# First mixer of a hybrid decoder: ten units multiply columns of x before the root mean square is known

## What is computed

```
def rmsnorm(x, g):
    y = x * rsqrt(mean(x * x, axis=-1, keepdims=True) + 1e-6)
    return y * g

def token_mixer(hn, ...):                      # hn = rmsnorm(x, ln1_g[l])
    p = hn @ w_in                              # 1024 x 5648
    xc, gb_c, gc_c, q, k, v, g_out, a_low, gate_a, gate_b = split(p)
    y_a = gb_c * short_conv(gc_c * xc, conv_w)             # three taps over the tokens
    log_a = log_sigmoid(a_low @ w_a2 + b_a) / 16
    o = gla(q * 64 ** -0.5, k, v, log_a)                   # 4 heads, chunks of 64 tokens
    y_b = rmsnorm(o, gla_norm_g) * silu(g_out)
    return (sigmoid(gate_a) * (y_a @ w_branch[0])
            + sigmoid(gate_b) * (y_b @ w_branch[1])) @ w_out
```

## Time and profile before

| what | value |
|---|---|
| median of 3 runs | 1408.72 us (1408.44 to 1408.95) |
| the profiled execution's own time | 1408.48 us |
| its span in the trace | 1406.7 us |
| TensorE busy | 1394.4 us, 99% |
| VectorE, ScalarE, GpSimd busy | 440.0, 301.6, 135.3 us |
| HBM | 462.7 MB moved, mean 329 GB/s |

### The profile page before, as it was taken

One profiled execution on the slowest core, in us unless ns is written; L12 is line 12 of the kernel. 1 busy time (PEld: TensorE's weight loads), 2 busy tenths in 40 slices (PEclk: granted clock), 3 DMA queues, 4 the chain that ended last, 5 costly groups with the idle time before them and its releaser, 6 DMA issues.

```text
span 1406.7 us, 34725 instructions
## 1 busy us (share of the span) xinstructions
PE 1394.4 (99%) x16039; PEld 870.3 (62%) x16039; DVE 440.0 (31%) x724; ACT 301.6 (21%) x425; POOL 135.3 (10%) x167
## 2 busy tenths in 40 slices
PE   9999999999999999999999999999999999999997
PEld 7999999999999983353353354354354344344344
DVE  6775775555777563110110110110110110110121
ACT  6554454444646430000000000000000000000000
POOL 2650000000463000000000000000000000000000
PEclk9999999999999999999999999999999999999999
DMA  9755566666565549999999999999999999999995
GB/s 329 253 180 181 180 195 195 207 204 190 173 201 195 192 160 358 417 418 419 417 419 419 416 419 411 412 420 410 412 421 410 413 420 408 414 421 408 421 420 202
DMA packets 132014, 462.73 MB, mean 329 GB/s; under 512 B 8531, under 2 KB 66545, under 8 KB 117538
## 3 DMA queue, kind: packets, MB, share of 16 engines
q1 hardware_dynamic: 126290, 449.87, 82.4%
q0 software_dynamic: 2448, 7.94, 1.5%
q10 hardware_dynamic: 3136, 2.75, 0.6%
HBM read 455.68 MB, written 4.86 MB: 327 GB/s over the span
## 4 chain that ended last, share of the span: by engine, by line
PE 96%; DVE 2%; issue 0%; DMA 0%; ACT 0%; POOL 0%; SPq 0%; POOLq 0%; DVEq 0%
PE banks L1602 95%; PE banks L1765 1%; DMA x<-in_x_dram 0%; DVE w_lo L819 0%; PE banks L1637 0%; DVE mem L1078 0%; POOL ors L1555 0%; DVE mem L855 0%; DVE mem L1115 0%; ACT mem L670 0%; PE banks L1867 0%; PE banks L1735 0%; PE banks L1798 0%; ACT mem L577 0%; DVE mem L1108 0%
## 5 line engine op out<-in xcount | busy, mean ns | idle before, releaser
L1602 PE MATMUL banks<-mem 128*32 128x448 f32 (+2 forms) x11712 | 878.4, 462 | 0.1
L1602 PEld LDWEIGHTS banks<-mem 128*32 128x32 f32 (+1 forms) x11712 | 381.5, 110 | 494.6 <-issue 377.1
L819 DVE TENSOR_TENSOR w_lo<-mem,w_hi 128x1024 fp32r<-128x1024 f32 x178 | 224.1, 1279 | 112.5 <-ACT w_hi L553 111.3
L1438 DVE TENSOR_TENSOR mem<-mem,banks 128x448 f32<-128x448 f32 x48 | 26.9, 616 | 716.2 <-PE banks L1602 716.2
L1602 PE MATMUL banks<-xt_hi,w_hi 128*128 128x256 f32 x832 | 230.1, 277 | 0.0
L1602 PE MATMUL banks<-xt_lo,w_hi 128*128 128x256 f32 x832 | 228.8, 275 | 0.0
L1602 PE MATMUL banks<-xt_hi,w_lo 128*128 128x256 f32 x832 | 228.8, 275 | 0.0
L553 ACT CAST w_hi<-mem 128x1024 fp32r<-128x1024 f32 x178 | 184.3, 1048 | 159.1 <-PE banks L1602 156.9
L1602 PEld LDWEIGHTS banks<-xt_hi,w_hi 128*128 128x128 f32 x832 | 159.6, 192 | 1.1 <-issue 0.3
L1602 PEld LDWEIGHTS banks<-xt_lo,w_hi 128*128 128x128 f32 x832 | 159.7, 192 | 0.3
L1602 PEld LDWEIGHTS banks<-xt_hi,w_lo 128*128 128x128 f32 x832 | 159.7, 192 | 0.0
(11 more groups left out here) (228 smaller groups left out, 703.3 us busy)
## 6 DMA issues: line engine op xcount, KB each, us to landing
mem<-in_eg_dram SPq DMA_DIRECT2D x128, 896.0 KB, 13.1
mem<-in_eu_dram SPq DMA_DIRECT2D x128, 896.0 KB, 12.9
mem<-in_ed_dram SPq DMA_DIRECT2D x112, 1024.0 KB, 15.2
mem<-in_w_in_dram SPq DMA_DIRECT2D x38, 1024.0 KB, 5.5
mem<-in_fg_dram SPq DMA_DIRECT2D x11, 1024.0 KB, 5.3
mem<-in_fu_dram SPq DMA_DIRECT2D x11, 1024.0 KB, 5.3
mem<-in_fd_dram SPq DMA_DIRECT2D x11, 1024.0 KB, 4.9
mem<-in_w_br_dram SPq DMA_DIRECT2D x8, 1024.0 KB, 5.5
```

Of the source, the lines that this page charges most:

```text
L819: nc.vector.tensor_tensor(w_lo[:, q % H, :], src, w_hi[:, q % H, :].bitcast(F32), ALU.subtract).then_inc(lo_done, 1)
L1438: nc.vector.tensor_tensor(h, h, by_pair(bank[3 + g]), ALU.mult).then_inc(ehf_done, 1)
L1602: return nc.tensor.matmul(out, lhs, rhs, start=first, stop=last, skip_group_check=True)
```

## The change

A second input `xt` holds x transposed on the host, eight blocks of 128 channels by 256 tokens, with the gain of the norm ahead. Its columns and the eight 256 KB parts of v's weights are loaded first, interleaved; the rows of x are loaded after the chunk of q. For l == 0, ten units (v, alow, q, k, xc0, xc1, gc0, gc1, gb0, gb1) multiply `x0_hi` and `x0_lo`, the split of x times gain, without r. r is made from the rows of x meanwhile, spread over the partitions by two matmuls into bank 7 (`spread_root`, between the halves of unit q) and copied to `rs_row`. It enters where the banks are read: v on ScalarE by r per partition; alow, q, k on VectorE times `rs_row`; xc0 and xc1 on VectorE times r squared (for xc and gc); the taps' result once more times r (for gb). ScalarE no longer reads q, k, xc0, xc1 in layer 0. For the units from go on, VectorE makes the normed columns (`normed`, eight multiplications of 128 x 256), ScalarE casts them (`normed_high`), VectorE subtracts (`normed_low`). TensorE's warm-up is eleven matmuls of zeros; the gain's spreading and the transposes of x go. The small parameter loads of GpSimd are issued after the second part of v has landed, the large ones after r.

```diff
@@ SyncE
+            columns(0, 0, KT + 2 * SEQ)
+            value_rows(0, 1, value_in[0])
+            value_rows(1, 1, value_in[1])
+            columns(1, KT + 2 * SEQ, KT + 4 * SEQ)
+            value_rows(2, 1, value_in[2])
+            value_rows(3, 1, raw_in[0])
+            columns(2, KT + 4 * SEQ, KT + 8 * SEQ)
+            value_rows(4, 2, value_in[3])
+            value_rows(6, 2, raw_in[1])
...
+                    if l == 0 and n == 2:
+                        for t in range(TB):
+                            sp.dma_start(x[:, t, :], x_d[0, t * P:(t + 1) * P, :]).then_inc(x_in[t], 16)
@@ ScalarE
+                    for kk in range(KT):
+                        weighed_high(kk)
+                        half_split(kk)
...
+                    until(H)
+                    norm_squares(0, (0, 2))
+                    until(H + 4)
...
+                if l == 0:
+                    after(2)
+                    normed_high(0)
+                    after(4)
+                    normed_high(1)
+                    after(5)
@@ VectorE
+                    for kk in range(KT):
+                        weighed_low(kk)
+                        half_low(kk)
...
                     until(H)
+                    own_half(0)
+                    own_half(1)
+                    dve.wait_ge(rs_full, 1)
+                    step(nc.vector.tensor_copy(rs_row, bank[7][:, 0:SEQ]))
...
+                    nc.vector.tensor_tensor(own_al, al_turned, rs_turned[0:2 * RANK, :, :], ALU.mult).then_inc(al_done, 1)
+                    step(nc.vector.tensor_tensor(rs_squared, rs_row, rs_row, ALU.mult))
+                    until(H + 2)
...
+                if l == 0:
+                    until(H + 3)
+                    src = full(l, "q")
+                    for h in range(HP):
+                        ins = nc.vector.scalar_tensor_tensor(...)
+                    ins.then_inc(q_done, 1)
+                    until(H + 4)
...
                 if l == 0:
+                    after(1)
+                    per_token(kT, full(l, "k"), rs_row).then_inc(k_done, 1)
+                    after(2)
+                    normed(0)
+                    after(3)
+                    for n in range(2):
+                        after(4 + n)
+                        per_token(cv[:, 2 * n:2 * n + 2, :], full(l, f"xc{n}"), rs_squared).then_inc(xc_done, 1)
+                        if n == 0:
+                            normed(1)
...
                 for n in range(2):
+                    if l == 0:
+                        normed_low(n)
                     after(6 + n)
...
+                if l == 0:
+                    step(nc.vector.tensor_tensor(cv[:, :, :], cv[:, :, :], rs_row.unsqueeze(1).to_broadcast([P, CB, SEQ]),
+                                                 ALU.mult))
@@ TensorE
-            keep_warm(3)
...
+            keep_warm(11)
             for l in range(DEPTH):
...
+                    for kk in range(KT):
+                        first_values(kk)
+                    low_rank(claim(l, "alow"), l, (x0_hi, x0_lo))
...
+                    channels(claim(l, "q"), base + 4, of=(x0_hi, x0_lo), between=spread_root)
```

More of the change, by code:

```diff
@@ L431, in unit_rows, with columns, value_rows @@
                 return rows(w_in_d[l], 0, KT, col, 256)
[L433 to L437, removed]
+            def columns(n, first, end):
+                sp.dma_start(g_xt[:, first:end], xt_d[:, first:end]).then_inc(xt_in[n], 16)
+            def value_rows(k0, nk, landed):
+                dst = raw(k0 // 4, k0 % 4 * 512, 512 * nk).rearrange("p (k n) -> p k n", k=nk)
+                sp.dma_start(dst, rows(w_in_d[0], k0, nk, C_V, 512)).then_inc(landed, 16)
+            columns(0, 0, KT + 2 * SEQ)
[7 more added lines that the diff above has]
+            value_rows(6, 2, raw_in[1])
             for l in range(DEPTH):
@@ L632, in _ @@
                 nc.scalar.activation(eb[:, :, :], bb[:, :, :], ACT.Exp, scale=1.0 / TAU).then_inc(eb_done, 1)
[L633 to L642, removed]
+                if l == 0:
[4 more added lines that the diff above has]
+                    after(5)
+                else:
+                    after(2)
+                    src = full(l, "q")
+                    nc.scalar.mul(halves(qT[:, :, :]), unturned(src[:, :], HP), DK ** -0.5).then_inc(q_done, 1)
+                    after(3)
+                    src = full(l, "k")
+                    nc.scalar.copy(halves(kT[:, :, :]), unturned(src[:, :], HP)).then_inc(k_done, 1)
+                    for n in range(2):
+                        after(4 + n)
+                        src = full(l, f"xc{n}")
+                        nc.scalar.copy(halves(cv[:, 2 * n:2 * n + 2, :]), unturned(src[:, :], 2)).then_inc(xc_done, 1)
                 for h in range(HP):
@@ new lines, in normed, with normed_low @@
+                    def normed(half):
+                        for kk in range(4 * half, 4 * half + 4):
+                            ins = nc.vector.scalar_tensor_tensor(out=x_cols[:, kk, :], in0=x_cols[:, kk, :],
+                                                                 scalar=g_cols[:, kk:kk + 1], in1=rs_row[:, :],
+                                                                 op0=ALU.mult, op1=ALU.mult)
+                        ins.then_inc(xn_made, 1)
+                    def normed_low(half):
+                        kk = 4 * half
+                        dve.wait_ge(xn_h, half + 1)
+                        nc.vector.tensor_tensor(xt_lo[:, kk:kk + 4, :], x_cols[:, kk:kk + 4, :],
+                                                xt_hi[:, kk:kk + 4, :].bitcast(F32), ALU.subtract).then_inc(xn_l, 1)
@@ L1639, in transposes, with channels @@
                 ins.then_inc(turned, 1)
-            def channels(out, q0, blocks=2, counts=(None, None), ready=None):
+            def channels(out, q0, blocks=2, counts=(None, None), ready=None, of=(xt_hi, xt_lo), between=None):
                 for half in range(2):
+                    if half and between is not None:
+                        between()
                     w = piece(q0 + half, counts[half])
```

228 lines of the change are left out of this document (129 added, 99 removed).

## The result

| | median of the runs | profiled execution | its span |
|---|---|---|---|
| before | 1408.47 us (1408.12 to 1408.95, 9 runs) | 1408.48 us | 1406.7 us |
| changed | 1412.94 us (1412.28 to 1413.59, 9 runs) | 1413.59 us | 1411.8 us |

The ratio is 1.0029, with a 95% interval of 1.0021 to 1.0038. The changed kernel is 4.5 us slower. The forecast was 1410.2, the range 1405.2 to 1414.0: the time is inside the range and 2.7 us above the point. It is above 1411.5, the prediction's bound for "slower", which had a chance of 0.32; "same" had 0.54.

What follows compares the result with a forecast made beforehand. TensorE, busy 99% of the span, was taken as the bound. A 4.7 us head start would be spent on VectorE's longer list, leaving TensorE 1.5 us late: 1408.48 + 1.5 = 1410.0, plus 0.24 for the median: 1410.2 us; range 1405.2 to 1414.0.

Steps and rivals of the forecast that it cites:

- same: Whole kernel: time neither below 1405.9 us (faster) nor above 1411.5 us (slower), chance 0.54.
- The start: Kernel start: first product at 5.7 us instead of 10.98, k starting at 26.3 instead of 31.05.
- head start: From the bias product z on: TensorE starts k 4.7 us sooner than in the kernel before.
- VectorE's list: First mixer, z to go's third piece: VectorE's old work, low parts, new work and waits run from 26.3 to 73.9.
- The wait before go's third piece: TensorE at go's third piece: one wait of some 5 us on the low part of piece 22.
- rival C: Start: r comes late, or landings or a low TensorE clock delay it; 1 to 3 us more, 1412.2, chance 0.11.
- The second chain: GpSimd, ScalarE and conv branch before the transposes: low part at 87.1, TensorE at 87.2; no further cost, no cover left.
- A: First mixer: VectorE keeps pace and the head start survives; 1404.0 with all of it, 1406.3 with half, chance 0.17.
- B: Second head pair's differences and taps: GpSimd and VectorE hold each other up, second exponential at 85, 1413.7, chance 0.15.
- D: Kernel start: the change gains nothing there, k no sooner than 29, VectorE's list 3 us later, 1413, chance 0.04.

Runs made afterwards that it cites:

- e1_warm: Changed kernel with 18 matmuls of zeros on TensorE between go's second and third pieces, filling its wait: 1410.44 us, ratio 1.0014 to the kernel before.
- e4_dose6: Kernel before with six extra, unused VectorE multiplications of 128 x 1024 behind the first mixer's taps: 1415.49 us, ratio 1.0049.
- e6_dose6_warm: Kernel before with e4_dose6's six extra VectorE multiplications plus 18 matmuls of zeros ahead of go's third piece: 1413.04 us, ratio 1.0033.
- e2_order: Changed kernel with ScalarE's two casts of x moved behind the casts of pieces 13 and 17: 1407.19 us, ratio 0.9990 to the kernel before.
- e7_tail: e5_both with VectorE's list behind the taps put in the order in which TensorE needs it: 1404.15 us, ratio 0.9973 to the kernel before.
- e4_dose4: Kernel before with four extra, unused VectorE multiplications of 128 x 1024 behind the first mixer's taps: 1410.70 us, ratio 1.0022.
- e3_late: Changed kernel with go multiplying columns without r (applied in ScalarE's silu) and all of `normed` behind the taps: 1408.00 us, ratio 0.9996 to the kernel before.
- e5_both: Changed kernel with e2_order's casts, e3_late's go, early `normed`, later `normed_low`, and GpSimd's chain started sooner: 1406.02 us, ratio 0.9984 to the kernel before.

## Why the prediction was right where it was, and what it missed

**The start: right.** Forecast: first product at 5.7, step 4 of v at 12.1, z's end at 26.3. The profiled execution had 6.50, 13.11 and 27.2, 0.8 to 1.0 us later, with TensorE standing for v's weights (L964): step 4's landed at 11.7 instead of 10.7. In the profiled executions of the five variants of the change z ended at 26.3 to 26.7. So a head start of 4.4 to 4.7 us is the usual one; 3.9 is this execution's, whose own time was 0.65 above the median. r cost TensorE next to nothing: its spreading began at 22.82, right behind a matmul that had started at 22.71.

**VectorE's list: right.** Forecast 47.6 us from z to the start of piece 22's low part (73.9 - 26.3), measured 47.3. Most terms stand one by one: two waits on ScalarE of 2.0 forecast, 2.06 measured; the eight multiplications 4.0 forecast, 2.30 + 1.66 measured; the reads 0.44 forecast, 0.38 measured; the taps' last product 1.33, within the 1.2 to 1.4. Others were off and cancelled: the fourteen low parts took 19.2 us and not 18.1, the wait behind the exponential 1.2 and not 0.8, while the taps took 7.3 and not 7.7 and the eight reads 3.0 and not 3.5. The wait before go's third piece was there: 4.5 us of the 5.3 that TensorE stood behind z in the first 100 us.

**The step that failed** is the sentence "so it stands some 6 us in all ... It goes on at 75.4 instead of 73.9: 1.5 us later than before". The time of the stand was priced, and what the stand does to the speed afterwards was not. TensorE goes on at 1.2 GHz, and two pieces of go that take 5.2 us take 8.2. By the trace the 4.9 us at 85.07 are 75.84 - 73.9 = 1.9 of lateness, where 1.5 was forecast, and 3.0 of clock, where nothing was. By the medians the 4.5 us are 2.0 (e1_warm over the kernel before) and 2.5 (the changed kernel over e1_warm). Without the fall, e1_warm came to 1410.44, 0.2 from the forecast of 1410.2 (part of this closeness is luck: the forecast added 0.24 for the median of three runs, which nine runs put at 1408.47, 0.01 below the profiled execution); e4_dose6 and e6_dose6_warm show 2.45 us, much the same, in the kernel before. The rows to see it by were there: the earlier trace rows showed 0.54 us for a matmul of zeros at the start, over twice the later 0.216, and the prediction used the lower level for rival C, at the start alone, and not behind a stand of its own making. The Trainium skill has the rule (TensorE: Matmul & The Clock Gate, HAM oscillation — how this bites in real kernels): a wait on data that is long enough between bursts of matmuls makes TensorE start the next burst at the lower clock. This trace agrees: 4.48 us of standing, then 0.50. It was the rule that spoke against this change, and the prediction weighed another one.

**The second chain: right, and without effect.** Forecast: GpSimd's last difference at 81, the low part at 87.1. Measured 81.1 and 87.3, by ScalarE's and VectorE's timelines of the changed kernel:

```profile
81.12 1.70 ACT L695 ACTIVATE mem<-mem 128x1792 f32<-128x1792 f32 x1 [14.63 <-POOL mem L1636]
```

```profile
86.07 1.22 DVE L1154 TENSOR_TENSOR area<-mem,area 128x1024 fp32r<-128x1024 f32 x1
```

But TensorE came to the transposes at 85.07 + 5.55 = 90.6 instead of 87.2, so the fall of the clock gave this chain 3 us of cover. Without the fall the cover is thin: in e1_warm the low part was done at 86.7 (85.52 + 1.22) and the transposes came at 87.35; in e2_order it was TensorE that waited, for 0.24 us.

**The rivals.** A (VectorE keeps pace, 1404.0) is not what the change did, but it is what e7_tail does, at 1404.15: the price of the full head start was right, and it took another order of VectorE's work and a go that multiplies the columns without r. B (GpSimd and VectorE hold each other up, 1413.7) gives the measured time from the wrong cause: the second exponential came at 81.1, not 83 or later. Had I looked at the time alone, B would have seemed shown. C and D did not occur: the spreading came at 22.8, before the mark of 23, and the first products ran at full speed.

**The chances.** With the 2.5 us of clock in the sum the point would have been 1412.7 and "slower" the likely case. The 0.54 for "same" rested on a sum in which this term was missing. The time is above the forecast's own range, 1408.0 to 1412.0; that it lies inside 1405.2 to 1414.0 is owed to the room left for B, whose mechanism did not occur, and so in part to luck.

## What to carry to other kernels

When a sum says that TensorE will stand still for several microseconds in one place, add what it does afterwards at the lower clock (2.3 to 3.0 us here for one stand of 4.5), and ask whether the stand can be cut or filled. A head start of TensorE is worth no more than the slack of the engine that feeds it, so put that engine's list in the order in which its results are needed, with everything that nobody waits for behind. A cast that waits for one engine and has another engine's work queued behind it stops both; here moving two casts of x behind two more casts of pieces each was worth 5.7 us, the clock's part included.

## What was not expected of the hardware

- Stands of TensorE of 1.7, 1.9 and 2.4 us in full work (e2_order, e4_dose4, e3_late) left the granted clock at 1.00 in the profiled executions; stands of 4.48 and 4.6 us (the changed kernel, e4_dose6) were followed by matmuls at the lower level, twelve of them in the changed kernel. Stands between these lengths were not tried, and four of the ten times of e4_dose4 are 2.2 us longer than the others without a trace that says why.
- In the changed kernel the eleven products of zeros from 1.03 to 6.1 were followed by real products at the full rate (6.50 on; the next start 0.21 us apart, from 6.82 to 7.03), while in the kernel before, zeros with waits between them were at the lower rate until 10.5 (three in 1.63 us). The record of the granted clock reads 1.00 in both kernels over this time, so the spacing of the matmuls is what shows it.
- GpSimd's operations that came early are not free to VectorE: `normed`'s four took 1.66 us with GpSimd idle and 3.61 us beside it (e5_both).
